# One-core transformer kernel: first weight tile in quarters, final normalisation shared by GpSimd and VectorE

## What is computed

```python
def rms_norm(x, g):
    xf = x.astype(jnp.float32)
    y = xf * lax.rsqrt(jnp.mean(xf * xf, axis=-1, keepdims=True) + NORM_EPS)
    return (y * g.astype(jnp.float32)).astype(x.dtype)

def diff_attn_layer(x, norm_g, w_in, ...):         # the first layer
    h = rms_norm(x, norm_g)
    q, k, v, gate = jnp.split(h @ w_in, 4, axis=-1)
    ...

def second_block(x, ..., final_norm):
    ...
        x = x + memory_cross_attention(rmsnorm(x, norm_xattn[l]), ...)
    return rmsnorm(x, final_norm)                  # the end of the kernel
```

## Time and profile before

| | us |
|---|---|
| timed runs | 2952.46 median of 3 (2948.04 to 2953.82) |
| span of the profiled execution, first to last instruction | 2947.0 |
| TensorE busy | 2876.8 (98%) |
| VectorE busy | 1243.9 (42%) |
| ScalarE busy | 975.6 (33%) |
| GpSimd busy | 1162.1 (39%) |
| first to last TensorE matmul of the weight stream | 9.3 to 2927.5 |
| mean granted TensorE clock | 0.994 of full |

### The profile page before, as it was taken

One profiled execution on the slowest core, in us unless ns is written; L12 is line 12 of the kernel. 1 busy time (PEld: TensorE's weight loads), 2 busy tenths in 40 slices (PEclk: granted clock), 3 DMA queues, 4 the chain that ended last, 5 costly groups with the idle time before them and its releaser, 6 DMA issues.

```text
span 2947.0 us, 41215 instructions
## 1 busy us (share of the span) xinstructions
PE 2876.8 (98%) x16960; PEld 2453.5 (83%) x16960; DVE 1243.9 (42%) x2202; ACT 975.6 (33%) x1433; POOL 1162.1 (39%) x888
## 2 busy tenths in 40 slices
PE   8999999999999988999999999999999999999997
PEld 8999999999999987777777778777777787787775
DVE  6333333333333347443434353632323234455546
ACT  4323222222313234244233344532332323234342
POOL 4343343434343433333434337434434343344342
PEclk9999999999999999999999999999999999999998
DMA  4122222222221212212222224222222221222221
GB/s 183 64 87 72 86 72 87 72 87 72 72 86 72 87 65 72 86 58 72 87 86 72 86 107 144 86 74 98 72 86 86 72 86 72 86 78 84 86 86 72
DMA packets 36942, 247.42 MB, mean 84 GB/s; under 512 B 3970, under 2 KB 4115, under 8 KB 8212
## 3 DMA queue, kind: packets, MB, share of 16 engines
q1 hardware_dynamic: 35728, 241.36, 23.2%
q10 hardware_dynamic: 1028, 3.44, 0.3%
HBM read 240.59 MB, written 4.19 MB: 83 GB/s over the span
## 4 chain that ended last, share of the span: by engine, by line
PE 89%; DVE 5%; ACT 2%; DVEq 1%; DMA 1%; POOL 1%; issue 1%; ACTq 0%; SPq 0%
PE pj L293 20%; PE pj L297 19%; PE pj L299 19%; PE pj L354 4%; PE pj L358 4%; PE pj L356 4%; PE pj L1026 2%; PE pj L1028 2%; PE pj L1027 2%; PE pa L543 1%; PE pa L505 1%; ACT wh L269 1%; POOL wl L2149 1%; PE pa L957 1%; DVE xl L401 1%; DVE arena L445 1%
## 5 line engine op out<-in xcount | busy, mean ns | idle before, releaser
L2149 POOL TENSOR_TENSOR wl<-raw,wh 128x512 fp32r<-128x512 f32 x884 | 1161.9, 1346 | 1749.7 <-ACT wh L269 1749.5
L293 PE MATMUL pj<-xh,wh 128*128 128x264 f32 (+2 forms) x3728 | 1086.8, 337 | 6.3 <-issue 3.9
L297 PE MATMUL pj<-xl,wh 128*128 128x264 f32 (+2 forms) x3728 | 1055.8, 329 | 5.8 <-DVE xl L401 5.8
L299 PE MATMUL pj<-xh,wl 128*128 128x264 f32 (+2 forms) x3728 | 1053.1, 329 | 0.0
L269 ACT ACTIVATE wh<-raw 128x2048 fp32r<-128x2048 f32 x221 | 423.1, 1914 | 1023.2 <-PE pj L299 641.1
L293 PEld LDWEIGHTS pj<-xh,wh 128*128 128x128 f32 x3728 | 632.8, 189 | 91.1 <-issue 24.3
L297 PEld LDWEIGHTS pj<-xl,wh 128*128 128x128 f32 x3728 | 631.4, 188 | 73.4 <-DVE xl L401 8.0
L299 PEld LDWEIGHTS pj<-xh,wl 128*128 128x128 f32 x3728 | 632.4, 189 | 64.2
L354 PE MATMUL pj<-oh,wh 128*128 128x264 f32 (+1 forms) x768 | 207.2, 324 | 11.5 <-DVE ol L794 8.7
L358 PE MATMUL pj<-oh,wl 128*128 128x264 f32 (+1 forms) x768 | 204.0, 320 | 0.0
L380 DVE TENSOR_TENSOR acc<-pj,acc 128x528 f32<-128x528 f32 (+1 forms) x208 | 145.6, 700 | 138.3 <-PE pj L358 137.3
(11 more groups left out here) (300 smaller groups left out, 2596.8 us busy)
## 6 DMA issues: line engine op xcount, KB each, us to landing
raw<-in_stream SPq DMA_DIRECT2D x221, 1024.0 KB, 4.8
acc<-in_x SPq DMA_DIRECT2D x8, 528.0 KB, 10.3
out_y<-acc SPq DMA_DIRECT2D x8, 512.0 KB, 2.9
arena<-in_mem ACTq DMA_DIRECT2D x2, 1024.0 KB, 6.3
cst<-in_cst SPq DMA_DIRECT2D x1, 448.0 KB, 13.7
cos<-in_cos_a SPq DMA_DIRECT2D x1, 264.0 KB, 13.8
sin<-in_sin_a SPq DMA_DIRECT2D x1, 264.0 KB, 14.0
cos<-in_cos_b ACTq DMA_DIRECT2D x1, 264.0 KB, 2.7
```

Of the source, the lines that this page charges most:

```text
L293: pe.matmul(pj[:, pu, b, 0:m], whk, xh[:, k, a:a + m], start=(k == 0), stop=False)
L297: pe.matmul(pj[:, pu, b, 0:m], whk, xl[:, k, a:a + m], start=False, stop=False)
L299: ins = pe.matmul(pj[:, pu, b, 0:m], wlk, xh[:, k, a:a + m], start=False, stop=(k == KD - 1))
L2149: pool.tensor_tensor(wl[:, j, at], raw[:, j, at], wh[:, j, at].bitcast(F32), ALU.subtract).then_inc(s_part if c < LO_PARTS - 1 else s_lo, 1)
```

## The change

At the start, the first tile is loaded in four quarters, interleaved with x0's first four parts; tile 1 is loaded behind the fourth of them. ACT rounds each quarter before the xh of the x0 part loaded after it; GpSimd makes each low quarter as soon as its high quarter is there; tile 1 is rounded after k = 7 instead of k = 4, tile 3 after all squares instead of at square 12. TensorE waits for the quarters one by one, and its lead becomes 9.

At the end, VectorE only adds the outputs. GpSimd sums the squares of k = 0 to 13, with a drain after each addition; the squares of 14 and 15 go to TensorE directly, which accumulates three products instead of one. ACT also multiplies slices 0 to 4 by their weight; it writes the reciprocal root twice, to PSUM for VectorE and to SBUF for GpSimd. VectorE scales slices 5 to 15, GpSimd slices 0 to 4, and nine stores follow in a fixed order.

```diff
--- before.py
+++ after.py
...
@@ -264,7 +268,7 @@
 
         def hi_part(act, t, par_t, used):
 
-            act.wait_ge(s_raw[par_t], t * 8 + 16 if par_t == 0 else t * 8 + 8)
+            act.wait_ge(s_raw[par_t], t * 8 if par_t == 0 else t * 8 + 8)
             act.wait_ge(s_out, used + 1)
             act.activation(wh[:, par_t, :], raw[:, par_t, :], ACT.Copy).then_inc(s_hi, 1)
 
@@ -304,7 +308,7 @@
                 for f in hooks[KD]:
                     f(pe)
 
-        FIRST_LEAD = 5
+        FIRST_LEAD = 9
 
         def proj_first_two(pe):
 
@@ -312,8 +316,11 @@
             for k in range(KD):
                 steps += [(0, k + FIRST_LEAD)] * (k + FIRST_LEAD < KD) + [(1, k)]
             for j, k in steps:
+                if j == 0 and k % (KD // LO_PARTS) == 0:
+                    pe.wait_ge(s_hi_q, k * LO_PARTS // KD + 1)
                 if k == 0:
-                    pe.wait_ge(s_hi, j + 1)
+                    if j == 1:
+                        pe.wait_ge(s_hi, 2)
                     pe.wait_ge(s_evac, j + 1)
                 if k == KD - KD // LO_PARTS:
                     pe.wait_ge(s_lo, j + 1)
@@ -449,17 +456,6 @@
         def stats_dve(dve, i, n, ssum, sq):
             for k in range(KD):
                 stats_tile(dve, i, k, n, ssum, sq)
-            dve.sem_inc(s_ssum, 1)
-
-        def add_stats(dve, u, pu0, i, ssum, sq):
-
-            for f in range(KD + 1):
-                if f < KD:
-                    dve.wait_ge(s_out, u + f + 2)
-                    dve.tensor_tensor(acc[:, f, 0:SEQ], ps_out((pu0 + f) % 2, SEQ), acc[:, f, 0:SEQ],
-                                      ALU.add).then_inc(s_evac, 1)
-                if f > 0:
-                    stats_tile(dve, i, f - 1, SEQ, ssum, sq)
             dve.sem_inc(s_ssum, 1)
 
         def stats_pe(pe, i, n, ssum):
@@ -2093,33 +2089,78 @@
                 dve.wait_ge(s_out, U_XA + 4 + k + 2)
                 dve.tensor_tensor(acc[:, k, 0:SEQ], ps_out((U_XA + k) % 2, SEQ), acc[:, k, 0:SEQ],
                                   ALU.add).then_inc(s_evac, 1)
-            add_stats(dve, U_XA + 20, U_XA % 2, 5, X_ssum, X_sq)
-
+            for f in range(KD):
+                dve.wait_ge(s_out, U_XA + 20 + f + 2)
+                dve.tensor_tensor(acc[:, f, 0:SEQ], ps_out((U_XA + f) % 2, SEQ), acc[:, f, 0:SEQ],
+                                  ALU.add).then_inc(s_evac, 1)
+            dve.drain()
+
+        F_POOL = 5
+        F_SUMS = KD - 2
+        F_rstd = bank[3]
 
         def final_act(act):
-            squares_act(act, 5, SEQ, X_sq, evacs=N_OUTS - KD)
-            rstd_act(act, 5, "eps6", SEQ)
+            for k in range(KD):
+                act.wait_ge(s_evac, N_OUTS - KD + k + 3)
+                square(act, 5, k, SEQ, X_sq)
+                if k < F_POOL:
+                    act.activation(acc[:, k, 0:SEQ], acc[:, k, 0:SEQ], ACT.Identity,
+                                   scale=par_col("final_norm_2", k)).then_inc(s_fing, 1)
+            act.wait_ge(s_ssps, 6)
+            act.activation(rstd[:, 0:SEQ], bank[2], ACT.Ln, scale=1.0 / D, bias=par_col("eps6"))
+            act.drain()
+            act.activation(F_rstd, rstd[:, 0:SEQ], ACT.Exp, scale=-0.5).then_inc(s_rstd, 1)
+            act.activation(rstd[:, 0:SEQ], rstd[:, 0:SEQ], ACT.Exp, scale=-0.5).then_inc(s_rstd, 1)
+
+        def final_pool(pool):
+            for k in range(1, F_SUMS):
+                pool.wait_ge(s_sq, 5 * KD + k + 1)
+                pool.tensor_tensor(X_ssum, X_sq[0][:, 0:SEQ] if k == 1 else X_ssum, X_sq[k % 2][:, 0:SEQ],
+                                   ALU.add).then_inc(s_squsd, 2 if k == 1 else 1)
+                pool.drain()
+            pool.sem_inc(s_ssum, 1)
+            pool.wait_ge(s_fing, F_POOL)
+            pool.wait_ge(s_rstd, 7)
+            for k in range(F_POOL):
+                pool.tensor_tensor(acc[:, k, 0:SEQ], acc[:, k, 0:SEQ], rstd[:, 0:SEQ], ALU.mult).then_inc(s_finp, 1)
 
         def final_pe(pe):
-            stats_pe(pe, 5, SEQ, X_ssum)
+            pe.wait_ge(s_ssum, 6)
+            pe.wait_ge(s_rstd, 5)
+            pe.matmul(bank[2], ones, X_ssum, start=True, stop=False)
+            for k in range(F_SUMS, KD):
+                pe.wait_ge(s_sq, 5 * KD + k + 1)
+                ins = pe.matmul(bank[2], ones, X_sq[k % 2][:, 0:SEQ], start=False, stop=(k == KD - 1))
+            ins.then_inc(s_ssps, 1)
 
         def final_dve(dve):
             dve.wait_ge(s_rstd, 6)
-            for k in range(KD):
+            for k in range(F_POOL, KD):
                 dve.scalar_tensor_tensor(acc[:, k, 0:SEQ], acc[:, k, 0:SEQ], par_col("final_norm_2", k),
-                                         rstd[:, 0:SEQ], ALU.mult, ALU.mult).then_inc(s_fin, 1)
+                                         F_rstd, ALU.mult, ALU.mult).then_inc(s_fin, 1)
+
+        def final_stores(sp):
+            stores = [(s_fin, 5, 7), (s_fin, 7, 9), (s_finp, 0, 2), (s_fin, 9, 11), (s_fin, 11, 13), (s_finp, 2, 4),
+                      (s_fin, 13, 15), (s_finp, 4, 5), (s_fin, 15, 16)]
+            for s, a, b in stores:
+                sp.wait_ge(s, b if s is s_finp else b - F_POOL)
+                sp.dma_start(dram["out"][:, a:b, :], acc[:, a:b, 0:SEQ]).then_inc(s_store, 16)
+            sp.wait_ge(s_store, 16 * len(stores))
 
         NT = dram["stream"].shape[0]
         block = ctx.enter_context(nc.Block())
 
         @block.sync
         def _(sp):
-            sp.dma_start(raw[:, 0, :], dram["stream"][0]).then_inc(s_raw[0], 16)
-            sp.dma_start(par[:, :], dram["par"]).then_inc(s_par, 16)
             for c in range(X_PARTS):
+                if c < LO_PARTS:
+                    at = slice(c * LO_COLS, (c + 1) * LO_COLS)
+                    sp.dma_start(raw[:, 0, at], dram["stream"][0][:, at]).then_inc(s_raw_q[c], 16)
+                if c == 0:
+                    sp.dma_start(par[:, :], dram["par"]).then_inc(s_par, 16)
                 k = slice(c * KD // X_PARTS, (c + 1) * KD // X_PARTS)
                 sp.dma_start(acc[:, k, :], dram["x0"][:, k, :]).then_inc(s_x0[c], 16)
-                if c == 1:
+                if c == LO_PARTS - 1:
                     sp.dma_start(raw[:, 1, :], dram["stream"][1]).then_inc(s_raw[1], 16)
             for name, dst in (("cst", cst[:, :]), ("cos_a", cos[:, :]), ("sin_a", sin[:, :])):
                 sp.dma_start(dst, dram[name]).then_inc(s_const, 16)
@@ -2134,17 +2175,17 @@
                 sp.wait_ge(s_hi, t - 1)
                 sp.wait_ge(s_lo, t - 1)
                 sp.dma_start(raw[:, t % 2, :], dram["stream"][t]).then_inc(s_raw[t % 2], 16)
-            for k in range(0, KD, 2):
-                sp.wait_ge(s_fin, k + 2)
-                sp.dma_start(dram["out"][:, k:k + 2, :], acc[:, k:k + 2, 0:SEQ]).then_inc(s_store, 16)
-            sp.wait_ge(s_store, 16 * KD // 2)
+            final_stores(sp)
 
         @block.gpsimd
         def _(pool):
 
             def lo_parts(t, j):
-                pool.wait_ge(s_hi, t + 1)
+                if t > 0:
+                    pool.wait_ge(s_hi, t + 1)
                 for c in range(LO_PARTS):
+                    if t == 0:
+                        pool.wait_ge(s_hi_q, c + 1)
                     at = slice(c * LO_COLS, (c + 1) * LO_COLS)
                     pool.tensor_tensor(wl[:, j, at], raw[:, j, at], wh[:, j, at].bitcast(F32),
                                        ALU.subtract).then_inc(s_part if c < LO_PARTS - 1 else s_lo, 1)
@@ -2154,19 +2195,28 @@
                     lo_parts(pair * 2 + j, j)
             for t in range(NT // 2 * 2, NT):
                 lo_parts(t, t % 2)
+            final_pool(pool)
 
         @block.scalar
         def _(act):
             act.preload_act_table_set("natural_log_exp_and_others")
-            hi_part(act, 0, 0, 0)
-            act.wait_ge(s_par, 16)
             for k in range(KD):
                 if k % (KD // X_PARTS) == 0:
-                    act.wait_ge(s_x0[k * X_PARTS // KD], 16)
+                    c = k * X_PARTS // KD
+                    if c < LO_PARTS:
+                        at = slice(c * LO_COLS, (c + 1) * LO_COLS)
+                        act.wait_ge(s_raw_q[c], 16)
+                        act.activation(wh[:, 0, at], raw[:, 0, at], ACT.Copy).then_inc(s_hi_q, 1)
+                    if c == LO_PARTS - 1:
+                        act.sem_inc(s_hi, 1)
+                    if c == 0:
+                        act.wait_ge(s_par, 16)
+                    act.wait_ge(s_x0[c], 16)
                 act.activation(xh[:, k, :], acc[:, k, :], ACT.Identity, scale=par_col("a_norm", k)).then_inc(s_xh, 1)
-                if k == 4:
+                if k == 2 * LO_PARTS - 1:
                     hi_part(act, 1, 1, 0)
-            squares_act(act, 0, T, A_sq, each={6: lambda: hi_part(act, 2, 0, 1), 12: lambda: hi_part(act, 3, 1, 2)})
+            squares_act(act, 0, T, A_sq, each={6: lambda: hi_part(act, 2, 0, 1)})
+            hi_part(act, 3, 1, 2)
             rstd_act(act, 0, "eps5", T)
 
```

(4 more changed lines are left out.)

## The result

The changed kernel takes 2956.84 us (median of 14 runs, 2950.99 to 2960.68), the kernel before 2950.09 (14 runs beside them, 2947.61 to 2953.82). The ratio is 1.0019, its 95% interval 1.0011 to 1.0027: some 6 us slower. The interval leaves 1 out; by the forecast's own measure, which counts up to 0.2% as no change, it is just within that. What the change was forecast to add, 2.1 us, was a third of what it added.

The account below looks back on a forecast made before the run. TensorE, busy 98% of the span, was taken as the bound, leaving only both ends to edit. Opening -1.2, later sum and products +1.3, clock +2.0 made +2.1 on 2952.46: 2954.6 us, range 2947.9 to 2959.3.

Parts of the forecast that it names:

- Case 5: Opening: quartered load does not start the work earlier, as start-up dominates; +3.3, 2955.8 us; chance 0.08.
- Tile 1, forecast to land near 14.0: Opening: tile 1, issued behind four quarters and four x0 parts, lands near 14.0 us, not 11.0.
- a quarter of 262 KB is 0.61 to 0.68 us at those rates: Opening: quarter loads move at 438 to 386 GB/s, so the first lands near 4.1 us instead of tile 0's 5.75.
- 112 matmuls left at 22.95: Opening: TensorE's last xl wait ends about 22.95 with 112 matmuls left, so tile 2 starts at 36.65 against 37.48.
- The 1.0 us stall goes: First layer's sum of squares: ready near 41.4, before TensorE asks at 43.3, so its 1.0 us wait disappears.
- The additions, forecast 1.38 apart: End: GpSimd's 13 drained additions take 1.38 us each (1.30 plus 0.08 drain), sum ready at 2929.4.
- ACT's squares and five scalings stay ahead: End: ACT's work, at most twice 0.69 us per k, never holds up GpSimd's additions.
- case 3: End: GpSimd bounds the tail, additions taking 1.68 us each; +6.6, 2959.1 us; chance 0.15.
- The main matmuls end no later than now: End: VectorE loses 16 stats operations; its PSUM and acc adds keep TensorE's pace, so matmuls end no later.
- The products, forecast 3.0 + 2.0: End: three fp32 products take 1.13 plus 1.88 us, and the lower clock adds 2.0 (0 to 2.6).
- The scaling worth nothing: End: sharing the scaling with GpSimd gains nothing, since stores need 10.8 us at 386 GB/s however fast scaling gets.
- Case 4: End: stores go faster with a backlog, 10.8 us shrinking to 9.6 at 438 GB/s; -4.2, 2948.3 us; chance 0.06.

Follow-up runs that it names:

- the idle products: The change's end alone (opening of before) plus five unread fp32 matmuls of constants before TensorE's wait for the sum; 2952.12 us, ratio 1.0009.

## Why the forecast was right and wrong

The time lay in the range, and the case of no measurable change (up to 0.2%) came true, with 0.19% by the ratio (the two medians are 0.23% apart). Much of that is luck. The forecast added 2.1 us to 2952.46, the median of three runs; over fourteen runs the kernel before has 2950.09. From there the 2.1 lead to 2952.2, 4.6 below the measured time, and a base 2.4 too high hid half of this. The 4.6 come from an opening with the wrong sign and from an end that was taken too small, in the additions and in the products above all.

- **The first product, forecast near 6.35: 6.51.** Right, and so was the landing of the first quarter and input. Case 5 fell.
- **Tile 1, forecast to land near 14.0: 16.1. Failed.** The step "a quarter of 262 KB is 0.61 to 0.68 us at those rates" took the loads' 438 and the stores' 386 GB/s as the two bounds for a quarter. Loads of 256 KB mostly lie well under both: 140 to 371 GB/s with them in flight, 233 to 315 when they stand in a row. The whole load, the only thing changed, brought the rate back to 398 and more and the first Ln to 45.81: that would have been -0.6.
  A rule of the Trainium skill speaks of this and I had passed it over: its page DMA: Bandwidth & Descriptors, Measured, has 1 MB at 341 GB/s and 64 KB at 138 (for loads issued by GpSimd) and says to batch loads to 1 MiB or more. The direction agrees with the runs, 398 to 418 GB/s with one load of 1 MB and 233 to 315 with four of 256 KB.
- **"112 matmuls left at 22.95", tile 2 at 36.65: 39.85. Failed with it.** Two stretches of TensorE in the changed kernel (length, busy, clock, DMA share, GB/s):

```profile
21.70:39.85 18.15, 18.14 (x136) 0.91 0.32 121
21.70:25.20 3.50, 3.49 (x16) 0.52 0.78 323
```

  From 21.7 to tile 2 it makes 136 matmuls, where the forecast's count leaves 122 at this point. ScalarE rounds tile 1 ahead of xh8, and tile 1 landed 2.1 us late. So TensorE waited 1.37 for xh8 until 18.79, and then for xl8 and xl9. What the late second quarter had cost before that was gone in this wait. The rest of the 3.2 us is the clock, but not all of the 1.5 by which 18.15 is over 136 x 0.1225 = 16.66, since at the high level TensorE would have waited for VectorE again. The row of xl11 (VectorE, start and length):

```profile
23.29 1.78 DVE L408 SCALAR_TENSOR_TENSOR xl<-acc,par,xh 128x528 fp32r<-128x528 f32 x1
```

  It ends at 25.07, 2.1 behind the forecast's 22.95. The forecast's 112 matmuls from there would start tile 2 at 38.8, an estimate; the measured 39.85 makes the clock worth 1.1. Its mechanism and place were right, its size was taken as 0.6.
  One reading in the forecast is not borne out by its own row. The pair at 12.39, with 0.64, was taken for the price of the lower level. But the granted clock of the kernel before is given as 1.00 there:

```profile
12.00:13.00 1.00, 1.00 (x5) 0.72 (x4) 1.00 (x2) 0.68 (x2) 1.00 (x2) 1.00 1.03 422
```

  TensorE's first matmuls run at 0.64 a pair in both kernels (until 13.5 before, 14.8 after), and the granted clock doesn't show why. The price of the lower level is right even so: the pair at 22.32 takes 0.64 where the granted clock is 0.52.
- **"The 1.0 us stall goes": it went, 1.2.** In part for another reason than forecast: tile 2 starts so late that the sum is ready. Moved alone, tile 3's rounding brings 0.45 and not 1.0, as VectorE's additions come next. That kernel has the first Ln at 45.93, where the three kernels with one load of tile 0 and the change's order have 45.78 to 46.15: TensorE's earlier start brings nothing that can be seen beside it.
- **The additions, forecast 1.38 apart: 1.46. Mis-sized.** The drain leaves 0.16 on GpSimd, not the 0.08 taken from VectorE. The twelve behind the first took 17.2 us in place of 16.6, and ahead of the second GpSimd waited 0.8 for ScalarE's square, which the step "ACT's squares and five scalings stay ahead" denied: the first addition reads both buffers of squares, so the third square could start only behind it; with 0.2 back from the first one and the last drain the chain was 1.3 us longer than forecast. What 1.46 decides is case 3: it stays under its 1.63.
- **"The main matmuls end no later than now": they end 1.5 earlier**, 21.3 us behind the last rounding and not 22.8. I had not looked at what the 16 operations cost VectorE. Order of time on VectorE in the kernel before:

```profile
2907.65 1.55 DVE L443 COPY arena<-tmp 128x512 f32<-128x512 f32 x1
2909.29 0.69 DVE L459 TENSOR_TENSOR acc<-pj,acc 128x512 f32<-128x512 f32 x1
2909.89 0.98 DVE L445 TENSOR_TENSOR arena<-arena 128x512 f32<-128x512 f32 x1
```

  While GpSimd makes the last wl, the copy takes 1.55 us and an addition 0.98, where one takes 0.68 once GpSimd is done; that the one causes the other isn't shown. The sum of PSUM and acc comes late, and TensorE falls behind. The change takes this away, and gains nothing, since what comes last is now GpSimd's chain: TensorE ends early and idles 4.76 us.
- **The products, forecast 3.0 + 2.0: 5.5.** The mechanism was right, and the idle products show it: 2.85 at the high clock. The clock was low under all six matmuls, so the upper bound of 2.6 was the value. But the profile of before was the wrong thing to hold this against in one way: its own product ran at the high clock, which the seven other profiles with an idle TensorE before one product don't repeat. They lose 0.7 to 0.9 there.
- **The scaling worth nothing: right.** 14.65 us against 14.36 from first scaling to end, with the stores at 378 and 390 GB/s at a share of 1.02 and 1.04; without the summation it is 14.4, and the time that of before. Case 4 fell: the backlog did not speed the stores, and the 436 GB/s of the Trainium skill (DMA: Bandwidth & Descriptors, Where 436 GB/s comes from) were reached by none of them.
- **The sum.** Opening +2.4 against the forecast, end +2.1 (1.3 the additions, 0.5 the products, 0.3 the last stores, all against the profile of before). This makes +6.6 over before in the profiles with the middle left out, and +6.75 in the medians. Against a usual last stage of before (43.4 to 43.8) it is +5.4 to +5.8, which is what the ratio says (1.0019 stands for 5.6 us). So 2956.8 lies between the forecast and case 3, whose mechanism, additions of 1.68, did not occur.

## What to carry to other kernels

Moving a sum off the engine that makes it is worth nothing unless the new chain, its drains counted, ends before the old one; and what it hands to TensorE after a pause must be priced at the low clock unless TensorE is kept busy. A first load cut into small pieces starts the work earlier and can delay everything behind it: cut the rounding, not the load. Edits of 1 to 2 us in a kernel whose unchanged middle differs by 11 us from one execution to the next can be read in the stage they touch, and hardly in the time.

## What the runs showed of the hardware

- Four loads of 256 KB at the start moved 233 to 315 GB/s at a DMA share of about 1 (140 in the worst microsecond when they alternate with inputs), one of 1 MB 398 to 418, two of 512 KB 219 to 365. From 3 to 8 us the means are 290 to 303, 409 and 319. Why loads in pieces of 2 KB are slower than stores in pieces of 2 KB (378 to 394) was not tried.
- Stores from buffers in one piece moved 394 to 404 GB/s from 2935 to 2943 us, those from rows with gaps 383 to 394 in the same stretches of the kernel before: 3% more.
- GpSimd's addition of 128x512 fp32 followed by a drain has a period of 1.46 us (1.30 and 0.16) in the three profiles read for it, beside VectorE's additions from PSUM, and of 1.42 behind the last of these. VectorE has 0.69 for the operation and 0.78 with a drain: a factor of 1.9 for both.
- The granted clock is 0.50 after 4.8 us of idle TensorE and 1.00 when products of no use fill the pause. After 2.5 us of idle TensorE it was 0.50 to 0.62 in the next microsecond in seven profiles and 1.00 in one.
- The kernel's first matmuls run at 0.64 a pair, as at the lower level, while the granted clock is shown as 1.00.
